# The fifth conditioning turn: multiplied and summed over feature tiles by VectorE, with only its partition sums on TensorE, and one tile of V placed behind the first heads' scores

## What is computed

```
m = silu(c) @ w + b                         # w: 1024 x 6144 for each layer
sh1, sc1, gt1, sh2, sc2, gt2 = split(m, 6)
h = x * (1 + sc1) + sh1
q = h @ b_wq ;  k, v = split(x @ kv_w) ;  logf = log_sigmoid(x @ f_w + f_b)
s = q k^T / 8 + cumsum(logf)_q - cumsum(logf)_k ;  o = softmax(s) v
x = LN(ALPHA * x + gt1 * (o @ b_wo)) ;  ... experts with sh2, sc2, gt2
```

## Time and profile before

| | us |
|---|---|
| three runs | 1017.19, 1016.65, 1010.38 |
| median of the runs | 1016.65 |
| the profiled execution's own time | 1011.46 |
| its span | 1009.8 |
| PE busy | 900.6 (89%) |
| DVE busy | 336.1 (33%) |
| ACT busy | 232.0 (23%) |
| POOL busy | 187.5 (19%) |

### The profile page before, as it was taken

One profiled execution on the slowest core, in us unless ns is written; L12 is line 12 of the kernel. 1 busy time (PEld: TensorE's weight loads), 2 busy tenths in 40 slices (PEclk: granted clock), 3 DMA queues, 4 the chain that ended last, 5 costly groups with the idle time before them and its releaser, 6 DMA issues.

```text
span 1009.8 us, 19113 instructions
## 1 busy us (share of the span) xinstructions
PE 900.6 (89%) x8206; PEld 620.2 (61%) x8206; DVE 336.1 (33%) x845; ACT 232.0 (23%) x528; POOL 187.5 (19%) x240
## 2 busy tenths in 40 slices
PE   3799999989999889999888899999999898997882
PEld 0577667869877657655445566756667576554451
DVE  0623341626435555211113502033222553111135
ACT  0221225223324232111000314133321322110003
POOL 0100002011372033321123210000000333211132
PEclk9799989989999897999998799979999979999995
DMA  9842221340245952599976987334738715999831
GB/s 368 365 167 84 83 84 33 147 170 5 86 154 199 427 207 70 216 416 422 425 304 234 413 321 284 121 130 153 270 124 344 285 62 202 413 420 424 337 112 47
DMA packets 29204, 230.45 MB, mean 228 GB/s; under 512 B 6816, under 2 KB 7360, under 8 KB 13984
## 3 DMA queue, kind: packets, MB, share of 16 engines
q1 hardware_dynamic: 19344, 208.66, 51.4%
q0 software_dynamic: 8064, 15.82, 4.3%
q10 hardware_dynamic: 1712, 4.75, 1.4%
HBM read 223.21 MB, written 16.32 MB: 237 GB/s over the span
## 4 chain that ended last, share of the span: by engine, by line
PE 70%; DMA 15%; DVE 7%; issue 3%; ACT 2%; POOL 1%; SPq 1%; POOLq 0%; ACTq 0%; DVEq 0%
PE ps L656 21%; PE ps L1004 9%; DMA arena<-in_experts 6%; PE ps L792 5%; DMA ring<-in_w 5%; PE ps L1051 4%; PE ps L677 4%; PE ps L638 3%; PE ps L799 3%; PE ps L1162 3%; DMA arena<-zbuf 2%; PE ps L746 2%; PE ps L984 2%; PE ps L805 1%; PE ps L719 1%
## 5 line engine op out<-in xcount | busy, mean ns | idle before, releaser
L656 PE MATMUL ps<-arena,ring 128*128 128x288 f32 x832 | 211.8, 415 | 4.9 <-DVE arena L1480 3.8
L656 PEld LDWEIGHTS ps<-arena,ring 128*128 128x128 f32 x832 | 159.5, 194 | 58.9 <-issue 12.3
L1004 PE MATMUL ps<-arena 128*64 128x256 f32 x960 | 113.9, 389 | 20.0 <-DMA arena<-in_experts 11.2
L1004 PEld LDWEIGHTS ps<-arena 128*64 128x64 f32 x960 | 74.1, 140 | 59.4 <-issue 18.8
L638 PE MATMUL ps<-con,arena 128*128 128x128 f32 (+3 forms) x398 | 66.8, 298 | 10.6 <-DVEq L1747 5.8
L638 PEld LDWEIGHTS ps<-con,arena 128*128 128x128 f32 (+3 forms) x398 | 46.6, 146 | 40.5 <-issue 21.7
L792 PE MATMUL ps<-arena 64*64 64x64 f32 x1888 | 63.4, 220 | 4.0 <-issue 3.0
L792 PEld LDWEIGHTS ps<-arena 64*64 64x64 f32 x1888 | 59.8, 136 | 10.1 <-issue 8.3
L643 PE MATMUL ps<-con 128*128 128x288 f32 x212 | 57.6, 430 | 2.3 <-DVE arena L1691 2.3
L1051 PE MATMUL ps<-arena 128*64 128x512 f32 x208 | 58.4, 599 | 0.8 <-DVE arena L1687 0.8
L2013 ACT ACTIVATE arena<-ps 128x128 f32<-128x128 f32 x36 | 10.0, 277 | 194.5 <-PE ps L1004 184.9
(11 more groups left out here) (306 smaller groups left out, 1228.4 us busy)
## 6 DMA issues: line engine op xcount, KB each, us to landing
arena<-in_experts SPq DMA_DIRECT2D x30, 2048.0 KB, 21.5
ring<-in_w SPq DMA_DIRECT2D x24, 2048.0 KB, 8.6
arena<-in_w SPq DMA_DIRECT2D x16, 2048.0 KB, 13.2
arena<-in_experts SPq DMA_DIRECT2D x30, 1024.0 KB, 15.9
ring<-in_experts SPq DMA_DIRECT2D x6, 2048.0 KB
ring<-in_experts SPq DMA_DIRECT2D x6, 1024.0 KB, 15.3
arena<-in_lora SPq DMA_DIRECT2D x1, 2560.0 KB, 41.4
hbuf<-arena SPq DMA_DIRECT2D x4, 512.0 KB, 3.1
```

What stands on the lines that cost most here:

```text
L656: last = mm(ps[:, tile % 4, 0:T], wslot[j][:, k, o * P:(o + 1) * P], rhs_at(k), start=k == 0, stop=k == KT - 1)
L1004: last = mm(ps[64 * j:64 * j + 64, 2 + b, 0:256], x(k), ewgu[slot][:, k, j * 256:(j + 1) * 256], start=k == 0, stop=k == KT - 1)
```

## The change

Turn 4 is no longer multiplied by PE. DVE takes each slot as it lies in SBUF and adds, for each stream, the two feature tiles times a scalar per partition into a row of 2048 per stream: `turn5[0]` and `turn5[1]`, in two activation buffers that are free at that time. That is four instructions of 128x2048 in each of four pieces, `turn5_piece(0)` to `(3)`, placed between the steps of the forget gates. What is left is the sum over the 128 partitions. PE does it in one piece of eight matmuls, `sum`, with a stationary `pick` of 128x32 that is one in column 0 (or 1) and zero elsewhere. It is the first entry of `ATT_PE`, and it waits for all four pieces. The slots of turn 4 leave the Q projection and `ATT_PE`; the tile `PV0` moves from behind `Tb0` to behind `S0`, with its copy `vPV0` on ACT before `sex0`. In SP's queue slot 3 now waits for DVE's first piece and stands ahead of half 1 of Q; turn 5's slot 0 waits for DVE's third piece.

```diff
-ASIDE = (..., "PV", "vPV")
+ASIDE = (..., "PV", "vPV", "sum")
 ATT_PE = """
-    S0:0 SS0:2 S1:4 ada34 ST0:0 Tb0:6 PV0:2 Ta0:3 cols4 VT0:4 Ta1:5 SS1:0 S2:2 S3:4 ada05 ST1:0
+    sum4 S0:0 PV0:6 SS0:2 S1:4 ST0:0 Tb0:6 Ta0:3 cols4 VT0:4 Ta1:5 SS1:0 S2:2 S3:4 ada05 ST1:0
 ATT_ACT = """
-    exa0 exb0 sex0 exa1 exb1 rows4 stc0 vPV0 tca0 ...
+    exa0 exb0 vPV0 sex0 exa1 exb1 rows4 stc0 tca0 ...
+        turn5 = [act_flat(i)[:, 0:2048] for i in (2, 5)]
+        pick = lnm2[:, 0:64]
# SP
             half(5, 0)
             sp.wait_ge(s["ada_done"], 4 * ADA_TURN)
             ada_weights(4, 2)
+            sp.wait_ge(s["turn5_in"], 1)
+            ada_weights(4, 3)
             half(5, 1)
-            sp.wait_ge(s["ada_done"], 4 * ADA_TURN + 1)
-            ada_weights(4, 3)
...
-                sp.wait_ge(s["ada_done"], 4 * ADA_TURN + 3 if j == 0 else 5 * ADA_TURN + j)
+                if j == 0:
+                    sp.wait_ge(s["turn5_in"], 3)
+                else:
+                    sp.wait_ge(s["ada_done"], 5 * ADA_TURN + j)
# PE
-            def next_turn(tile):
-                if tile < ADA_TURN - 1:
-                    ada_slot(4, tile)
-            project(5, lambda k: Hh[:, k, :], then=next_turn)
+            project(5, lambda k: Hh[:, k, :])
...
+                if name == "sum":
+                    pe.wait_ge(s["turn5_in"], ADA_TURN)
+                    pe.wait_ge(s["mod_ready"], 4 * ADA_TURN)
+                    pe.wait_ge(s["f_neg"], 1)
+                    for q in range(4):
+                        for st in range(2):
+                            last = mm(ps[32 * q:32 * q + 32, ADA_BANK[4], :], pick[:, 32 * st:32 * st + 32],
+                                      turn5[st][:, q * 512:(q + 1) * 512], start=st == 0, stop=st == 1)
+                    last.then_inc(s["ada_done"], ADA_TURN)
+                    return
# DVE
+            def turn5_piece(j):
+                dve.wait_ge(s[f"ada_in{j}"], 16 * 5)
+                w = ada_buf(4, j).rearrange("p (k n) -> p k n", k=2)
+                for k in range(2):
+                    for st in range(2):
+                        x = c2[:, 2 * j + k, st:st + 1]
+                        if j or k:
+                            link(V.scalar_tensor_tensor(turn5[st], w[:, k, :], x, turn5[st], ALU.mult, ALU.add))
+                        else:
+                            link(V.tensor_scalar(turn5[st], w[:, k, :], x, None, ALU.mult))
+                dve.sem_inc(s["turn5_in"], 1)
             parts(3)
             dve.wait_ge(s["mod_ready"], 4 * ADA_TURN)
             one_more((1, 1))
             dve.sem_inc(s["mod_go"], 1)
+            dve.wait_ge(s["x_ready"], 2 * KT)
+            link(V.memset(pick, 0))
+            for st in range(2):
+                link(V.memset(pick[:, 33 * st:33 * st + 1], 1.0))
+            turn5_piece(0)
             dve.wait_ge(s["f_mm"], 1)
             link(V.tensor_scalar(lft[0][0:80, :], ps[0:80, 7, 0:T], small[0:80, 0:1], None, ALU.add))
             dve.sem_inc(s["f_neg"], 1)
+            turn5_piece(1)
             dve.wait_ge(s["f_act"], 1)
...          # scan of the prompt, nF
+            turn5_piece(2)
             dve.wait_ge(s["attn_small"], 16)
...          # scan of the cache, nFS
             dve.sem_inc(s["nf_ready"], 1)
+            turn5_piece(3)
```

More of the change, by code:

```diff
@@ L139 @@
 WKV_PE = [job.split(":")[0] for job in WKV_PE]
-ASIDE = ("ada0", "ada1", "ada2", "ada3", "rows", "cols", "mod", "PV", "vPV")
+ASIDE = ("ada0", "ada1", "ada2", "ada3", "rows", "cols", "mod", "PV", "vPV", "sum")
 class Turns:
@@ L203 @@
 ATT_ACT = """
-    exa0 exb0 sex0 exa1 exb1 rows4 stc0 vPV0 tca0 vVT0 tca1 sex1 exb2 exa2 exa3 stc1 exb3 oc0 tca2 vPV1
+    exa0 exb0 vPV0 sex0 exa1 exb1 rows4 stc0 tca0 vVT0 tca1 sex1 exb2 exa2 exa3 stc1 exb3 oc0 tca2 vPV1
     vVT1 exb4 soc0 exa4 oc1 tca3 vPV2 exb5 exa5 vVT2 oc2 sex2 tca4 vPV3 vVT3 exa6 rows5 soc1
@@ L444, in build @@
         names = """consts_in con_in x_in lora_in rw_in wready0 wready1
-            ada_in0 ada_in1 ada_in2 ada_in3 mod_go xx_edge ada_done ada_rows ada_t csil_ready
+            ada_in0 ada_in1 ada_in2 ada_in3 mod_go xx_edge ada_done turn5_in ada_rows ada_t csil_ready
             csig_done mod_ready h_ready mix_ready tile_done tile_free shift_out lora1_done lora1_act
```

## The result

Over 20 runs each, the changed kernel has a median of 1016.25 us (1010.32 to 1021.67), the kernel before 1012.25 us (1006.95 to 1019.4). The ratio is 1.0038, with a 95% interval of 1.0020 to 1.0056: 0.4% slower, some 4 us. The forecast was 3.7 us faster than the profiled execution of before. The time lies in the range, but the sign is wrong. All ratios here are taken over the executions within 1.5% of the fastest of the same version; longer ones are one of twelve in e2, two in e4 and three each in e5 and e6, and the profile of e6 is one of these.

The account below looks back on a forecast made before the run. PE was taken to bound the stretch from the K projection to the attention's end. SS1 starting 6.0 us sooner (clock back with the sum) or 1.4 (halfway through PV0) gave a middle of 3.7: 1011.46 to 1007.8 us, range 1001 to 1019.

Parts of the forecast that it names:

- Q ends 6.2 us sooner.: Q projection on PE: three slots of 2.05 us leave, so it ends at 646.3 instead of 652.45.
- DVE's pieces, 2.29 us an instruction, last one done at 648.8, wait 2.5 us.: DVE's multiplications during Q: pieces of 9.3 us, the first 7.3; PE, done at 646.3, idles 2.5 us before the sum.
- Piece 0 hidden, `f_neg` not late, `nf_ready` late but hidden.: DVE around the forget gates: piece 0 ends 7 us before they come; nf_ready is 14.5 us later at no cost.
- Slot 3 ahead of half 1 of Q.: DMA queue: half 1 lands by 630.2 at worst, Q's tile 4 needs it at 630.8; hidden by 0.6 us.
- The rival of the late transfer: Q's weights: slot 3 ahead of half 1 makes tile 4 late; 1008 to 1013 us, chance 0.05.
- 1.3 us before `ST0` where the fourth slot stood.: PE behind S1: with the slot gone, ST0 waits about 1.3 us for DVE's snm0.
- 0.7 us before `cols4`.: PE behind the transposes after S1: cols4 waits 0.7 us more for ACT's copy of the bank.
- The clock falls in the new wait.: PE's wait before the sum: an idle gap of 2.5 us was expected to bring half clock from there.
- It comes back with the sum or halfway through `PV0`; I take the middle.: Clock after the wait: full again with the sum gains 6.0 us, halfway through PV0 1.4; middle taken, 3.7 us.
- Slower by a fall behind `S1`.: Rival: idle transposes bring half clock for SS1 to S3, price 8 to 11 us; 1015.5 to 1018.5, chance 0.25.
- No fall at all,: Rival: the wait before the sum is too short to lower the clock; 7.9 us gained, 1003.6, chance 0.20.
- The dip cost 6.1 us: First heads' scores in the profile before: half clock from about 655.7 to 669.2 cost 2.1 + 2.7 + 0.8 + 0.5 us.

Follow-up runs that it names:

- e2: Changed kernel with 16 useless matmuls of 128x288 filling PE's wait before the sum; ratio to the kernel before 1.0018 (0.9981 to 1.0054).
- e4: Changed kernel with two of the four instructions of DVE's last piece left out, so PE has no wait before the sum; ratio to before 0.9963.
- e5: Changed kernel with 7 useless matmuls of 128x288 filling PE's wait before the sum; ratio to the kernel before 0.9984 (0.9960 to 1.0009).
- e6: Changed kernel with PV0 put back behind Tb0 and the sum still first; ratio to the kernel before 1.0043 (1.0010 to 1.0076).
- e1: Changed kernel with the sum moved back behind S1 and PV0 back behind Tb0; ratio to the kernel before 0.9952, median 1007.91 against 1011.15 us.

## Why the prediction was wrong

Step by step, as it was put:

- *Q ends 6.2 us sooner.* Right: Q takes 31.2 us instead of 37.4, and e1 gains 6.1 us in all.
- *DVE's pieces, 2.29 us an instruction, last one done at 648.8, wait 2.5 us.* Undersized. The instruction took 2.35 to 2.36 us, and there is 0.1 to 0.2 us around each piece. Over three pieces that is 1.1 us, all of it PE's, plus the handoff: 3.77 us. Inside the bound given (up to 2.56 us).
- *Piece 0 hidden, `f_neg` not late, `nf_ready` late but hidden.* Right: DVE was idle for 6.95 us before the forget gates, and `nf_ready` at 643.97 is 6 us ahead of Q's end.
- *Slot 3 ahead of half 1 of Q.* Right. The slowest landing in the ring rose from 10.8 to 14.8 us, and Q didn't stop. The rival of the late transfer is out.
- *1.3 us before `ST0` where the fourth slot stood.* Right: 1.42.
- *0.7 us before `cols4`.* About right: 0.49 us in e5 at full clock, hidden by the slower transposes in the change.
- *The clock falls in the new wait.* Right, three times out of three. *It comes back with the sum or halfway through `PV0`; I take the middle.* Close to the late end, each time: half clock for 13.7 us, and 3.6 + 6.1 + 5.2 = 14.9 us for the sum, `S0` and `PV0`, which take 1.9 + 3.4 + 4.1 in e5; the middle was 13.3. The old fall, read from 655.7 to "about 669.2", lasted as long: by the 0.61 in the earlier trace rows it ended at 669.4. It had ended within the fourth slot, from which the prediction drew that the sum might end the new one; the sum has the same matmuls, and none of the three profiles shows it.
- *Slower by a fall behind `S1`.* The fall is there in all three profiles, but only for 3.3 us, and `SS1` to `S3` run at full clock. It costs 0.9 us (21 transposes in 3.97 us against 3.12 in e5, its wait of 0.49 included), not 8 to 11. In e2 and e5, with the same wait of 1.42 us but no fall before it, the clock stayed at full there. The rival had the sign and not the mechanism.
- *No fall at all,* which the Trainium skill (TensorE: Matmul & The Clock Gate, the table "Why this matters for your kernels") would have given for a gap of 2.5 us: not the case. The gap was 3.8 us, but by the clock means of the wait (0.79, 0.83 and 0.89) the clock was at half 2.2, 2.4 and 3.0 us behind Q's end. In two of three profiles a gap of 2.5 us would thus not have been short enough, which speaks against the page.

**Two steps failed, and it took both to turn the sign.** The first is the base of the sum. "The dip cost 6.1 us", and "so I expect `SS0` and `S1` outside the dip": the 6.1 us were booked as belonging to the kernel before and as curable by the change. Two of three profiles of that kernel don't have them, so its stretch is on average 61.4 us and not 65.5: 4.1 us that were not there to be gained. The second is the length of what the change brings. The forecast made the stretch 3.7 us shorter than 65.5, and it was 0.2 shorter. The 3.5 us between are the wait (3.77 instead of 2.5, 1.3 us), the half clock, of which it took the middle (14.9 instead of 13.3 us for sum, `S0` and `PV0`, 1.6), and the part from `S1` to `SS1` (5.4 instead of 4.8, 0.6). With the right base alone the forecast would have been 0.4 us slower, which is no difference; with the right lengths alone, 0.2 us faster. Both together give 65.3 against 61.4, 3.9 us slower.

Against a kernel whose clock stays up, the measured pieces are: slots -6.2, wait +3.8, `S0`'s old wait -0.5, sum beyond its slot +1.8, `S0` at half +2.7, `PV0` +1.3, `snm0` +1.4, transposes and `cols4` +1.5. That is +5.8 us, and 59.4 + 5.8 = 65.2, where the stretch shows 65.3. This is an account of what was measured, not a test of it; the test is e5. The prediction noted that the runs shown spread by "about one dip's cost", but used it only for where the median might stand. It did not ask whether that dip was itself what varied from run to run, made the rarer case its reference, and so a certain fall looked no dearer than the old one.

What stays open: the mean loss fits a fall in one of three executions of the kernel before, but three profiles don't fix that share, and why the clock falls behind half an idle microsecond in one profile and not in five others, and behind none at all in e4, isn't settled. The clock also falls around 740 to 750 us, near the fourth sample heads' scores, for 6.8 us in the second and third profile of the kernel before and in the first of the changed one; these differences are not attributed to the change.

## What to carry to other kernels

A clock fall in one profile can be a draw and not a property of the kernel: before it is booked as cost or gain, profile the same kernel again. Here a wait of 3.8 us was followed by a fall in four profiles of four (the changed kernel and e6), one of 0.5 us in one of six, and e4's fall had none ahead of it. Work moved to an idle engine is free only as far as its result isn't needed; put the piece that needs it last among what PE can do meanwhile, and a loss of 0.4% becomes a gain of 0.5 to 0.7%. Where a slot that covered a wait is removed, put the new piece there: the sum behind `S1` covers the 1.42 us that every version without a piece in that place waits.

## What the runs showed of the hardware that was not expected

The wait of 3.8 us brought 13.7 us of half clock in each of the three profiles of the changed kernel, and 23.8 us in the one profile in which no projection tile followed the first scores (e6). But the fall behind 0.5 us of idle time in the first profile of the kernel before lasted 13.7 us as well (655.7 to 669.4), and the one behind none in e4 10.2 us. So the length of a fall did not go by the gap ahead of it here; in the first of these PE was busy all through. In the changed kernel the half clock cost more than the wait itself, 6.4 us beside 3.8. Filling the wait with useless matmuls was faster than idling, 58.9 us for the stretch against 65.3 to 65.8. A scalar-tensor-tensor on 128x2048 float32 took 2.35 us, about 3% above the slope of the shorter and longer two-input instructions.
